# Fused decoder step, end of the expert stage: two pairs added by one-hot products, rows loaded behind the weights, sums and scalings on three engines

## The chip, the cores and the metric

One Trainium2 chip, one of its cores. The metric is the device time of one execution in microseconds (us), smaller is better. The kernel before took 805.71 us (median of 3 runs, 805.52 to 807.05). Engines are named TensorE (PE in the profile, PEld for its weight loads), VectorE (DVE), ScalarE (ACT), GpSimd (POOL) and SyncE (SP, which here only issues DMAs).

## The reference, cut to what matters

One decoder layer for 576 tokens (512 of a prompt, 64 of samples) of width 1024, all fp32. The change touches only its last part: the mixture of experts and the final norm.

```python
def hier_moe(x, lp):                       # 32 experts, each token takes 2 of them
    ...
    combine = ...                          # (tokens, experts): the two weights of each token, else 0
    y = jnp.zeros_like(xt)
    for e in range(N_EXPERTS):
        h = jax.nn.silu(xt @ lp['w_e_gate'][e]) * (xt @ lp['w_e_up'][e])
        y = y + combine[:, e:e + 1] * (h @ lp['w_e_down'][e])
    return y.reshape(shp)
# in the layer, then after it
x = x + hier_moe(rmsnorm(x, lp['norm2_g']), lp)
y = rmsnorm(x, final_norm_g)               # x * rsqrt(mean(x*x) + eps) * gain
```

## The kernel before, in words

The program has one instruction stream per engine, written out by hand, with semaphores between them. Everything up to the router is left alone by the change (some semaphores are merged). At the end stand the expert stage and the final sums.

**Expert stage.** The 32 experts are run as 16 pairs (`NPAIR`), pair i being experts 2i and 2i+1. Each expert of a pair has 64 slots for tokens, so a pair is 128 rows. For pair i: GpSimd gathers the 128 token rows by an indirect DMA (L2625), TensorE turns them (`turn_rows`), multiplies with gate and up weights in two halves (`gate_up(i, 0)`, `gate_up(i, 1)`), ScalarE and VectorE make the hidden values (`gate`, `hidden`), TensorE turns those (`turn_hidden`) and multiplies with the down weights (`down(i)`, into PSUM buffer 3). VectorE copies the result out (`result(i)`, L2404) and GpSimd scatters the 128 rows to a DRAM tensor `expert_rows` (`scatter(i)`, L2634), by (choice, token). The weights, 6 MB per pair, come in chunks of 1 MB through 20 slots of SBUF, issued by SyncE (L511) as `ew_used` says that slots are free. If an expert has more than 64 tokens, an overflow part runs behind `If(overflow(...) > 0)`; in these runs it is skipped.

**The last pair.** Pair 15 isn't scattered. A one-hot matrix `L_SEL` (slot to token) and the weight of each slot `L_W` are made beforehand: VectorE builds matrices (`weigh_slots`, L2416 to L2424), TensorE sums them (`slot_weights`, in `body(13)`), VectorE reads the sum and builds the one-hot matrix (`pick_slots`). The result of `down(15)` is split in a high part (ScalarE, L1679) and a low part (VectorE, L2455), and TensorE adds both to the tokens with `picked`: 4 products of 128x512 for each of the 5 tiles of tokens.

**The end.** The tokens stand in 5 tiles `H_AT[t]` (t = 0 has 64 rows, the others 128). When `scatter(14)` has landed, SyncE issues 10 loads (`load_results`, L554): for each tile the row of its first choice and of its second. VectorE adds them with the weights `R_W0` and `R_W1` (tiles 0 and 1: L2493, L2494, then L2496 adds TensorE's PSUM; tiles 2, 3, 4: TensorE also adds the tile itself and its first choice as products with diagonal matrices, and L2500 adds the second choice). ScalarE squares and sums each tile and takes the root (L1688, L1690), VectorE inverts it and scales the tile by it and by the gain (`finish`, L2510, L2511), and SyncE stores the tile (L581), in the order 0 to 4.

Of the kernel before, what the change touches and what calls it, by code (L numbers as in the profile page):

```python
# [150 lines left out]
M_JUNK = O_A + 14400  # L151
# [16 lines left out]

def piece_of(n, i):

    for off, dims, first, many in SLOTS_E[n % NSLOT]:
# [8 lines left out]
def landed(n):  # L180

    k = n % NSLOT // 2 * 2
    return 16 * (len(SLOTS_E[k]) + len(SLOTS_E[k + 1])) * (n // NSLOT + 1)
# [17 lines left out]
N_MAIN = 6 * NPAIR  # L201
# [26 lines left out]
PE_TILES = {2: 0, 3: 3, 4: 2}  # L228
PICKED = {0: 2, 1: 1, **PE_TILES}
L_HI, L_LO, L_SEL, L_W = M_YO + 1024, M_XGT, M_XG + 1024, R_SS + 13  # L230
# [106 lines left out]
def build(nc, small, ssm, h0, xT, x, memT, mem, wstream, wexp, bias, sbias, skT, sv, mkT, mv, cache_k, cache_v,  # L337
# [18 lines left out]
    with ExitStack() as ctx:  # L356
# [21 lines left out]
        def pat(i, off, *dims, p0=0, pn=P):  # L378
# [14 lines left out]
        x_sq, consts_set, gx_ready, xn_ready = sem("x_sq"), sem("consts_set"), sem("gx_ready"), sem("xn_ready")  # L393
# [8 lines left out]
        qm_sb, memn, memsq, mkv_sb, kmT_sb, thg_sb, zz_ready = (sem(n) for n in (  # L402
            "qm_sb", "memn", "memsq", "mkv_sb", "kmT_sb", "thg_sb", "zz_ready"))
# [5 lines left out]
        ss2, rt_ready, x2_ready, x2T_sb, gate_d, gate_e, m_onehot, oh_ready, idx_ready = (  # L409
            sem(n) for n in ("ss2", "rt_ready", "x2_ready", "x2T_sb", "gate_d", "gate_e", "m_onehot", "oh_ready", "idx_ready"))  # L410
# [13 lines left out]
        ssf, rootf, y_sum, y_done, y_st = (sem(n) for n in ("ssf", "rootf", "y_sum", "y_done", "y_st"))  # L424
        more_ps, diag_w = sem("more_ps"), sem("diag_w")
        cleared, slot_oh, slot_ps, y_half, y_hi, y_lo = (sem(n) for n in (
            "cleared", "slot_oh", "slot_ps", "y_half", "y_hi", "y_lo"))
        out_st = sem("out_st")
# [45 lines left out]
        def _(sp):  # L474
# [28 lines left out]
            def chunk(n, e):  # L503
# [3 lines left out]
                for off, dims, first, many in SLOTS_E[n % NSLOT]:  # L507
# [3 lines left out]
                    sp.dma_start(at(off, *dims), src).then_inc(ew_ready[n % NSLOT // 2], 16)  # L511
# [31 lines left out]
            for n in range(19, N_MAIN):  # L543
                wait_pos(sp, ew_used, n + 1 - NSLOT)
# [5 lines left out]
            def load_results():  # L550
                for t in range(TT):
# [7 lines left out]
            sp.wait_ge(y_sent[0], 16 * (NPAIR // 2))  # L559
            sp.wait_ge(y_sent[1], 16 * (NPAIR // 2 - 1))  # L560
            sp.wait_ge(ew_used, CHUNK_AT["d", NPAIR - 2, 0, 1] + 1)
            load_results()
            with sp.If(overflow(sp) > 0):
                for t in range(TT):
                    sp.wait_ge(ld_row[t], 48 if t < TT - 1 else 64)
                for n in range(N_MAIN, len(CHUNKS)):
# [2209 lines left out]
```

## Time and profile before

| what | us |
|---|---|
| median of the runs | 805.71 |
| the profiled execution's own time | 806.09 |
| its span, first to last instruction | 804.3 |
| TensorE busy (matmul) | 758.0 |
| VectorE busy | 392.3 |
| ScalarE busy | 244.2 |
| GpSimd busy | 74.8 |

A span is what the trace covers; the execution's own time is 1.8 us longer. Matmul records overlap, so a busy TensorE isn't TensorE at its peak. From about 560 us on the page shows 412 to 428 GB/s of DMA in every slice of 20 us, until 764 us; the slice of 764 to 784 us has 304 and the last 236.

### The profile page before, as it was taken

The numbers are of one execution on the slowest core, as the hardware profiler recorded it, in microseconds if no ns is written. First come the engines' busy times: TensorE is split into PE (matmuls) and PEld (weight loads), VectorE is DVE, ScalarE is ACT, GpSimd is POOL, SyncE is SP. The second block draws the span as 40 slices with busy tenths as digits, with TensorE's granted clock in tenths as the row PEclk, the third lists the DMA queues.
The fourth block names the chain that finished last, engine by engine and source line by source line (L and its number), as shares of the span: only waits on it lengthen the run. The fifth ranks groups of instructions, "written<-read, shape, count | busy, mean of one in ns | idle before, by whom it ended". The sixth has DMA issues, their size and how long they took to land.

```text
span 804.3 us, 12111 instructions
## 1 busy us (share of the span) xinstructions
PE 758.0 (94%) x4993; PEld 579.4 (72%) x4993; DVE 392.3 (49%) x734; ACT 244.2 (30%) x429; POOL 74.8 (9%) x104
## 2 busy tenths in 40 slices
PE   8999999999999999999999999999999997778875
PEld 6889999999998766789999989886333332323332
DVE  3599828994632757466244367546121121113237
ACT  1552333213473534552243252112111111100113
POOL 0100022001003010100000010011112211111100
PEclk9999999999999999999999999999999999999998
DMA  9668135623335454210241388269999999999986
GB/s 343 238 190 324 63 109 81 150 77 155 98 133 211 184 215 152 105 53 2 105 161 64 158 325 333 79 268 350 412 421 424 421 421 424 421 422 428 420 304 236
DMA packets 38731, 190.62 MB, mean 237 GB/s; under 512 B 5994, under 2 KB 7546, under 8 KB 22968
## 3 DMA queue, kind: packets, MB, share of 16 engines
q1 hardware_dynamic: 24288, 148.22, 46.7%
q0 software_dynamic: 11200, 34.98, 13.0%
q10 hardware_dynamic: 3184, 6.60, 2.2%
q8 instruction: 41, 0.67, 0.3%
q14 instruction: 18, 0.15, 0.1%
HBM read 176.17 MB, written 21.41 MB: 246 GB/s over the span
## 4 chain that ended last, share of the span: by engine, by line
PE 79%; DMA 11%; ACT 5%; DVE 3%; issue 1%; ACTq 0%; SPq 0%; DVEq 0%
PE ps L611 75%; DMA sb<-in_wexp 10%; PE ps L622 4%; ACT sr L1408 1%; ACT sb L1492 1%; DMA sb<-in_xT 1%; ACT sb L1421 1%; ACT sb L1293 1%; DVE sb L2421 0%; DVE sb L2063 0%; DVE sb L2028 0%; DVE sb L2500 0%; DVE sb L2049 0%; DVE sr L2001 0%; ACT sb L1437 0%
## 5 line engine op out<-in xcount | busy, mean ns | idle before, releaser
L611 PE MATMUL ps<-sb 128*64 128x512 f32 (+16 forms) x2216 | 385.0, 432 | 32.3 <-DMA sb<-in_wexp 21.1
L611 PEld LDWEIGHTS ps<-sb 128*64 128x64 f32 (+6 forms) x2216 | 219.4, 157 | 170.9 <-issue 133.5
L611 PE MATMUL ps<-sr 128*128 128x288 f32 (+2 forms) x2372 | 336.9, 302 | 4.2 <-DVE sr L2455 2.4
L611 PEld LDWEIGHTS ps<-sr 128*128 128x128 f32 x2372 | 320.2, 188 | 14.9 <-issue 8.1
L622 PEld LDWEIGHTS ps<-sb 128*128 128x128 f32 (+3 forms) x405 | 41.8, 140 | 30.0 <-issue 26.5
L2396 DVE SCALAR_TENSOR_TENSOR sb<-sb,ps 128x256 f32<-128x256 f32 x16 | 6.7, 421 | 112.0 <-ACT sb L1660 112.0
L622 PE MATMUL ps<-sb 128*128 128x128 f32 (+3 forms) x405 | 52.6, 269 | 1.5 <-DVE sb L2090 0.6
L2404 DVE COPY sb<-ps 128x1024 f32<-128x1024 f32 x15 | 18.4, 1225 | 61.4 <-PE ps L611 61.4
L2136 DVE TENSOR_TENSOR sr<-sb,sr 128x2048 fp32r<-128x2048 f32 (+1 forms) x15 | 34.7, 2324 | 27.4 <-ACT sr L1403 17.6
L1293 ACT ACTIVATE sb<-ps 128x576 f32<-128x576 f32 (+4 forms) x29 | 22.9, 789 | 70.4 <-PE ps L611 50.4
L2122 DVE SCALAR_TENSOR_TENSOR sb<-sb,ps 128x576 f32<-128x576 f32 x24 | 18.1, 753 | 53.3 <-PE ps L611 53.3
L1655 ACT ACTIVATE sb<-ps 128x256 f32<-128x256 f32 x16 | 6.1, 384 | 106.1 <-PE ps L622 99.8
L2634 POOL DMA_INDIRECT expert_rows<-sb x15 | 15.7, 1047 | 172.1 <-DVE sb L2404 157.6
L1660 ACT ACTIVATE sb<-ps 128x256 f32<-128x256 f32 x16 | 6.1, 383 | 75.2 <-PE ps L611 75.2
L1403 ACT ACTIVATE sr<-sb 128x2048 fp32r<-128x2048 f32 x14 | 26.7, 1912 | 1.9 <-ACT sb L1531 1.2
L1531 ACT ACTIVATE sb<-ps 128x288 f32<-128x288 f32 x24 | 9.6, 408 | 53.7 <-PE ps L611 49.0
L2001 DVE TENSOR_TENSOR sr<-sb,sr 128x2048 fp32r<-128x2048 f32 x6 | 13.7, 2291 | 24.0 <-ACT sr L1408 13.0
L1797 DVE TENSOR_TENSOR sr<-sb,sr 128x2048 fp32r<-128x2048 f32 x10 | 22.9, 2290 | 3.2 <-ACT sr L1315 2.9
L1470 ACT ACTIVATE sb<-sb 128x256 f32<-128x256 f32 (+2 forms) x36 | 16.6, 462 | 24.1 <-DVE sb L2066 24.1
L1315 ACT ACTIVATE sr<-sb 128x2048 fp32r<-128x2048 f32 x10 | 19.0, 1908 | 0.6 <-ACT sb L1293 0.2
L1324 ACT ACTIVATE sb<-ps 128x576 f32<-128x576 f32 x8 | 5.2, 652 | 44.4 <-PE ps L611 44.4
L1650 ACT ACTIVATE sb<-ps 128x1024 f32<-128x1024 f32 x15 | 15.4, 1024 | 9.5 <-PE ps L622 9.5
(275 smaller groups left out, 484.5 us busy)
## 6 DMA issues: line engine op xcount, KB each, us to landing
sb<-in_wexp SPq DMA_DIRECT2D x91, 1024.0 KB, 23.5
sb<-in_wstream SPq DMA_DIRECT2D x33, 1024.0 KB, 5.1
expert_rows<-sb ACTq DMA_DIRECT2D x1, 4608.0 KB, 21.3
sb<-in_mkT POOLq DMA_DIRECT2D x8, 512.0 KB, 9.7
sb<-in_mv POOLq DMA_DIRECT2D x8, 512.0 KB, 6.3
sb<-expert_rows SPq DMA_DIRECT2D x8, 512.0 KB, 8.1
sb<-in_wexp SPq DMA_DIRECT2D x5, 768.0 KB
sb<-in_x SPq DMA_DIRECT2D x4, 512.0 KB, 14.3
```

Source lines behind the costliest of these rows:

```text
L611: return signed(nc.tensor.matmul(*a, **kw))
L622: return signed(nc.tensor.transpose(*a))
L1293: c.free(fn(dst, src, ACT.Copy, **kw), job)
L1315: fn(r32(EARLY_HI[b], WB), at(raw_at(b), (1, WB)), ACT.Copy).then_inc(hi_ready, 1)
L1403: fn(r32(high_at(block), 2048), at(raw_at(b), (1, WB)), ACT.Copy).then_inc(hi_ready, 1)
L1470: fn(at(sc + m * 256, (1, keys)), at(sc + m * 256, (1, keys)), ACT.Exp, bias=at(stat(n, 1) + m, (1, 1)), accum_out=at(stat(n, 3) + m, (1, 1)))
L1650: fn(at(M_XGT, (1, 1024)), pat(0, 0, (1, 1024)), ACT.Copy).then_inc(xT_sb, 1)
L1797: v.tensor_tensor(r32(raw_at(b), WB), at(raw_at(b), (1, WB)), r32(EARLY_HI[b], WB).bitcast(F32), ALU.subtract).then_inc(lo_ready, 1)
L2122: c.free(v.scalar_tensor_tensor(g2, g2, 1.0, pat(pair(name), 0, (512, 2), (1, TH)), ALU.add, ALU.mult), name)
L2136: v.tensor_tensor(r32(src, n), at(src, (1, n)), r32(hi, n).bitcast(F32), ALU.subtract).then_inc(lo_ready, 1)
L2404: v.tensor_copy(at(M_YO + (i % 2) * 1024, (1, 1024)), pat(3, 0, (1, 1024))).then_inc(y_copied, 1)
L2634: pool.indirect_dma_start(out=y_d[:, :], out_offset=bass.IndirectOffsetOnAxis(at(M_IDX + i, (1, 1)).bitcast(U32), 0), in_=at(M_YO + (i % 2 ...
```

## The change

Pairs 14 and 15 (`LAST`) are both added by one-hot products; `scatter(14)` and the copy before it are gone. The row loads then wait for `scatter(13)` only, and come in the order 0, 3, 1, 2, 4. What is summed where also changes: `sum_rows` (tiles 0 and 3) stands on VectorE ahead of the low parts of pair 15; tile 1's rows are scaled by ScalarE and added by GpSimd; tiles 0 and 1 get their final scaling from ScalarE (by the root) and GpSimd (by the gain). Only tile 2 still gets its rows by TensorE's diagonal products. On TensorE the common path stands in its own `If`, and the overflow part behind it. Merged semaphores, moved buffers and slot numbers of the overflow part are left out here.

```diff
@@ sync
             def load_results():
-                for t in range(TT):
+                for t in (0, 3, 1, 2, 4):
...
-            sp.wait_ge(y_sent[0], 16 * (NPAIR // 2))
-            sp.wait_ge(y_sent[1], 16 * (NPAIR // 2 - 1))
-            sp.wait_ge(ew_used, CHUNK_AT["d", NPAIR - 2, 0, 1] + 1)
+            for k in range(2):
+                sp.wait_ge(y_sent[k], 16 * (NPAIR // 2 - 1))
+            sp.wait_ge(ew_used, CHUNK_AT["gu", NPAIR - 2, 1, 1] + 1)
             load_results()
...
-                sp.wait_ge(y_done, t + 1)
+                sp.wait_ge(*((gained, t + 2) if t < 2 else (y_done, t + 1)))
                 sp.dma_start(out_y[WTOK[t]:WTOK[t] + R, :], ...
@@ tensor
             def down(i):
                 pe.wait_ge(hT_sb, i + 1)
-                wait_pos(pe, y_copied, i)
+                wait_pos(pe, y_copied, copies(i - 1))
+                if i == LAST[1]:
+                    pe.wait_ge(y_lo, 2)
...
             def body(i, first, last):
...
-                if i == NPAIR - 3:
-                    slot_weights()
+                if i == NPAIR - 4:
+                    slot_weights(1)
+                if i == NPAIR - 2:
+                    slot_weights(3)
+                if last:
+                    own_rows(2)
                 gate_up(i, 1)
                 if last:
-                    own_rows(2)
+                    pe.wait_ge(y_lo, 2)
+                    for half in range(2):
+                        picked(LAST[0], 2, half)
                     turn_hidden(i)
...
                 down(i1 - 1)
+                for t in range(2):
+                    for half in range(2):
+                        picked(LAST[0], t, half, start=True)
...
+            def sums():
+                pe.wait_ge(y_lo, 3)
+                for t in range(3):
+                    for half in range(2):
+                        if t == 0 and half:
+                            pe.wait_ge(y_lo, 4)
+                        last = picked(LAST[1], t, half, stop=(t < 2))
+                    if t < 2:
+                        last.then_inc(more_ps, 1)
+                pe.wait_ge(diag_w, 1)
+                first_choice(2)
+                for half in range(2):
+                    picked(LAST[0], 3, half, start=True)
+                    last = picked(LAST[1], 3, half, stop=True)
+                last.then_inc(more_ps, 1)
+                pe.wait_ge(y_sum, 1)
+                for half in range(2):
+                    picked(LAST[0], 4, half, start=True)
+                    last = picked(LAST[1], 4, half, stop=True)
+                last.then_inc(more_ps, 1)
@@ scalar
+            def high_rows(j):
+                act.wait_ge(slot_oh, 4 if j == LAST[0] else 6)
+                for half in range(2):
+                    act.wait_ge(*((y_ps, j + 1) if half else (y_half, j - LAST[0] + 1)))
+                    fn(r32(L_HI[j] + half * 512, 512), pat(3, half * 512, (1, 512)), ACT.Copy, scale=at(L_W[j], (1, 1)))\
+                        .then_inc(y_hi, 1)
...
+            high_rows(LAST[1])
+            act.wait_ge(ld_row[1], 48)
+            for k, w in enumerate((R_W0, R_W1)):
+                rows_1 = at(A_WG[1] + k * D, (1, D), pn=WROWS[1])
+                fn(rows_1, rows_1, ACT.Copy, scale=at(w + 1, (1, 1), pn=WROWS[1])).then_inc(scaled, 1)
...
                 fn(ss, ss, ACT.Sqrt, scale=1.0 / D, bias=at(O_EPS, (1, 1), pn=R)).then_inc(rootf, 1)
+                if t in (1, 2):
+                    h = at(H_AT[t - 1], (1, D), pn=WROWS[t - 1])
+                    act.wait_ge(y_done, t)
+                    fn(h, h, ACT.Copy, scale=at(R_SS + 7 + t, (1, 1), pn=WROWS[t - 1])).then_inc(scaled, 1)
@@ vector
             def pairs(i0, i1):
...
+                    if i == NPAIR - 5:
+                        weigh_slots(LAST[0])
                     if i == NPAIR - 4:
                         weight_diagonals()
-                        weigh_slots()
+                    if i == NPAIR - 3:
+                        pick_weight(LAST[0])
+                        weigh_slots(LAST[1])
                     if i == NPAIR - 2:
-                        pick_slots()
-                result(i1 - 2)
+                        pick_tokens(LAST[0])
+                        pick_weight(LAST[1])
+                        pick_tokens(LAST[1])
+                if i1 == NPAIR:
+                    low_rows(LAST[0])
+                else:
+                    result(i1 - 2)
                 hidden(i1 - 1)
+            def add_first(t, rows_landed):     # A_WG = A_WG * R_W0 + H_AT, waits for ld_row[t]
+            def add_second(t):                 # A_WG = A_WG(second) * R_W1 + A_WG
+            def sum_rows(rows_landed):
+                add_first(0, rows_landed)
+                add_second(0)
+                add_first(3, rows_landed)
+                c.settle()
             pairs(0, NPAIR)
+            sum_rows(48)
+            dve.sem_inc(added, 1)
+            low_rows(LAST[1])
...
             def combine(t):
+                if t not in PE_TILES:
+                    dve.wait_ge(more_ps, t + 1)
+                    c.do(v.tensor_tensor(h, pat(PICKED[t], 0, (1, D), pn=R), at(A_WG[t], (1, D), pn=R), ALU.add), y_sum)
+                    return
...
             def finish(t):
                 dve.wait_ge(rootf, t + 1)
-                if t == 0:
+                if t < 2:
+                    c.do(v.reciprocal(ss, ss), y_done)
+                    return
...
+            add_second(3)
             combine(0)
+            add_first(4, 64)
+            add_second(4)
+            finish(0)
+            dve.wait_ge(gained, 1)
             combine(1)
-            finish(0)
-            finish(1)
             combine(2)
             combine(3)
+            finish(1)
+            combine(4)
             finish(2)
-            combine(4)
             finish(3)
             finish(4)
@@ gpsimd
-                    if i > i0:
+                    if i > i0 and i - 1 != LAST[0]:
                         scatter(i - 1)
             pairs(0, NPAIR)
+            rows_1 = [at(A_WG[1] + k * D, (1, D), pn=WROWS[1]) for k in range(2)]
+            for k in range(2):
+                pool.wait_ge(scaled, k + 1)
+                if k:
+                    pool.wait_ge(own_sum, 1)
+                nc.gpsimd.tensor_tensor(rows_1[0], rows_1[k], rows_1[0] if k else at(H_AT[1], (1, D), pn=WROWS[1]), ALU.add)\
+                    .then_inc(gained if k else own_sum, 1)
...
+            pool.wait_ge(ld["gf"], 16)
+            for t in range(2):
+                h = at(H_AT[t], (1, D), pn=WROWS[t])
+                pool.wait_ge(scaled, t + 3)
+                nc.gpsimd.tensor_tensor(h, h, at(M_GF, (1, D), pn=WROWS[t]), ALU.mult).then_inc(gained, 1)
```

## Rows read from the trace of the kernel before

**Rows 1.** The chain that ended last: start us, length us, engine and line.

```profile
746.60 21.92 DMA sb<-in_wexp
768.65 5.57 PE ps L611 x20
779.34 0.76 DVE sr L2455
799.97 1.28 DVE sb L2511
```

**Rows 2.** Stretches: length, busy us (instructions) per engine, PEclk, DMA share, GB/s.

```profile
768.50:771.50 3.00, 2.85 (x14) 1.26 (x16) 0.00 (x0) 0.00 (x0) 0.98 (x1) 1.00 0.99 415
771.50:775.00 3.50, 3.03 (x12) 1.04 (x10) 0.84 (x2) 0.77 (x2) 0.00 (x0) 1.00 0.42 171
775.00:776.50 1.50, 1.50 (x8) 0.54 (x10) 0.00 (x0) 0.00 (x0) 0.00 (x0) 1.00 0.00 0
```

**Rows 3.** Three lots of row loads: ns each, first and last issue, then landing.

```profile
L554 SPq DMA_DIRECT2D sb<-expert_rows x2: 455/526/597, 775.4 to 775.9; - x2
DMA to landing us min/median/max: 3.5/4.6/5.7
...
L554 SPq DMA_DIRECT2D sb<-expert_rows x3: 432/432/1614, 777.2 to 778.1; - x3
DMA to landing us min/median/max: 6.7/7.0/8.9
...
L554 SPq DMA_DIRECT2D sb<-expert_rows x2: 431/456/482, 780.8 to 781.3; - x2
DMA to landing us min/median/max: 8.9/9.7/10.5
```

**Rows 4.** The scatter of pair 13: timeline row, its landing.

```profile
758.60 1.53 POOL L2634 DMA_INDIRECT expert_rows<-sb x1 [12.06 <-DVE sb L2404]
DMA to landing us min/median/max: 8.4/8.4/8.4
```

**Rows 5.** Timeline of GpSimd and VectorE around 541 us; L2275's five instructions (min/median/max ns).

```profile
540.92 2.36 POOL L2613 TENSOR_TENSOR sb<-sb 128x1024 f32<-128x1024 f32 x1 [10.75 <-DVEq L2206]
540.92 0.22 DVE L2271 TENSOR_TENSOR sb<-sb,ps 128x64 f32<-128x64 f32 x1
541.43 2.00 DVE L2275 TENSOR_TENSOR sb<-sb 128x128 f32<-128x128 f32 x1
L2275 DVE TENSOR_TENSOR sb<-sb x5: 283/294/1997, 497.0 to 550.8; 128x128 f32<-128x128 f32 x4, 64x128 f32<-64x128 f32 x1
```

**Rows 6.** VectorE's groups from 776 us on: busy us, mean ns, idle before.

```profile
L2511 DVE SCALAR_TENSOR_TENSOR sb<-sb 128x1024 f32<-128x1024 f32 x4 | 5.1, 1284 | 0.1
L2496 DVE TENSOR_TENSOR sb<-ps,sb 128x1024 f32<-128x1024 f32 x1 | 1.2, 1224 | 0.0
L2510 DVE RECIPROCAL sb<-sb 128x1 f32<-128x1 f32 x4 | 0.6, 160 | 0.3 <-ACT sb L1690 0.3
```

**Rows 7.** ScalarE: square and root of one tile, table load; the copy with a scale (L1641).

```profile
779.56 1.28 ACT L1683 ACT_TABLE_LOAD x1 [0.25 <-issue]
785.47 1.06 ACT L1688 ACTIVATE sb<-sb 64x1024 f32<-64x1024 f32 x1 [4.41 <-DVE sb L2496]
786.65 0.29 ACT L1690 ACTIVATE sb<-sb 64x1 f32<-64x1 f32 x1
L1641 ACT ACTIVATE sb<-sb x1: 1148/1148/1148, 545.0 to 545.0; 128x1024 f32<-128x1024 f32 x1
```

**Rows 8.** The stores of the result.

```profile
DMA to landing us min/median/max: 2.6/2.6/2.9
```

**Rows 9.** TensorE at its slot weights, the next wait for weights, and a stretch between.

```profile
732.20 6.64 PE L611 MATMUL ps<-sb 64*128 64x1 f32 x26 [1.98 <-DVEq L2425]
752.88 3.65 PE L611 MATMUL ps<-sb 128*64 128x512 f32 x16 [0.91 <-DMA sb<-in_wexp]
735.00:736.00 1.00, 1.00 (x4) 0.24 (x2) 0.00 (x0) 0.00 (x0) 0.00 (x0) 0.50 0.99 414
```

More of the change, by code:

```diff
@@ L227, with copies, sent @@
 R_DG = R_SEL[0]
[L228 to L230 removed]
+PE_TILES = {2: 0}
+PICKED = {0: 2, 1: 1, 2: 0, 3: 3, 4: 2}
+LAST = (NPAIR - 2, NPAIR - 1)
+L_HI, L_LO = (dict(zip(LAST, places)) for places in ((O_A + 12544, M_YO + 1024), (O_A + 13568, M_XGT)))
+L_SEL, L_W = (dict(zip(LAST, places)) for places in ((O_X, M_XG + 1024), (R_SS + 5, R_SS + 13)))
+def copies(i):
+    return i + 1 if i < LAST[0] else max(LAST[0], i)
+def sent(i):
+    return i // 2 - (i > LAST[0] and i % 2 == 0)
 L_ONE, L_TMP = O_TH + 2048, R_TB + 32
@@ L1171, in own_rows, with picked, slot_weights @@
                        stop=not start)
-            def slot_weights():
-                pe.wait_ge(slot_oh, 1)
+            def picked(j, t, half, start=False, stop=False):
+                for k, y in enumerate((L_HI[j], L_LO[j])):
+                    last = mm(pat(PICKED[t], half * 512, (1, 512)), r32(L_SEL[j] + WTOK[t], 128), r32(y + half * 512, 512),
+                              start=(start and k == 0), stop=(stop and k == 1))
+                return last
+            def slot_weights(step):
+                pe.wait_ge(slot_oh, step)
                 for t in range(TT):
@@ L1212, in pairs, with first_choice @@
                 down(i1 - 1)
+                for t in range(2):
+                    for half in range(2):
+                        picked(LAST[0], t, half, start=True)
             pairs(0, NPAIR)
-            with pe.If(overflow(pe) > 0):
+            def first_choice(t):
+                pe.wait_ge(ld_row[t], 48 if t < TT - 1 else 64)
+                for half in range(2):
+                    last = mm(pat(PE_TILES[t], half * 512, (1, 512)), at(R_DG + (t - 2) * 128, (1, 128)),
+                              at(A_WG[t] + half * 512, (1, 512)), start=False, stop=True)
+                last.then_inc(more_ps, 1)
[18 more added lines that the diff above has]
+                    last = picked(LAST[1], 4, half, stop=True)
+                last.then_inc(more_ps, 1)
+            many, left = overflow(pe), list(owed)
+            with pe.If(many < 1):
+                sums()
+            with pe.If(many > 0):
+                owed[:] = left
                 own_rows(2, start=False)
+                for t in range(2):
+                    for half in range(2):
+                        picked(LAST[0], t, half, stop=True)
                 pe.wait_ge(oh2_ready, 1)
@@ L2484, in _ @@
                     dve.wait_ge(ld_row[t], 80 if t < TT - 1 else 96)
+                sum_rows(80)
+                add_first(1, 80)
+                add_second(1)
             c = main
```

166 lines of the change are left out of this document (77 added, 89 removed).

## Prediction

> **What bounds the kernel now.** I read the chain of waits first. Up to 768.5 us it lies on the weights' DMA (21.92 us in its last stretch), then TensorE runs the last pair, and from 780 us on it goes through the end's sums to VectorE's last scaling, over at 799.97 + 1.28 = 801.25 us [rows 1]. The last store lands 2.6 us later [rows 8]; the 0.45 us left to 804.3 are its issue and the close. So nothing ahead of the weights' end can gain, unless it reduces what the DMA moves. The stretches say when the DMA is free: it moves 415 GB/s until 771.5 us, 171 until 775 us, and nothing until 776.5 us [rows 2]. It stands still because the row loads are issued only at 775.42 us, after pair 14's scatter. Their landings set when VectorE can begin: the second load of tile 0 was issued at 775.9 us and landed 5.7 us later, at 781.6 us; the second load of the next tile landed at 783.9 (777.2 + 6.7), the third tile's at 787.0 (778.1 + 8.9), the last tile's at 791.8 us (781.3 + 10.5) [rows 3]. From 781.6 to 801.25 us VectorE has hardly a gap. So 19.7 us of VectorE's work, begun by the row loads, is what the change attacks.
>
> **The change, step by step.**
>
> *Row loads.* They now wait for pair 13's scatter, landed at 758.60 + 8.4 = 767.0 us [rows 4], and queue behind the weights and the gain. From 768.5 to 775 us the DMA moved 415 x 3.0 + 171 x 3.5 = 1.84 MB [rows 2]; 0.52 MB of it was pair 14's scatter, now gone. The rest at 415 GB/s takes 3.2 us, so the rows' data begin at about 771.6 us, not 776.5. I move each place in the order 5 us forward: tile 0 at 776.6, tile 3 (second place now) at 778.9, tile 1 (third) at 782.0, tile 4 at 786.8 us. Bounds: 4 us forward if pair 13's scatter is late, 7 us if the queue behind the weights hides the ramp that the first landing shows (3.5 us from issue).
>
> *VectorE ahead of the last low parts.* `sum_rows`, with waits for the rows of tiles 0 and 3, stands in front of `low_rows(15)`: behind these waits queue the low parts, and for those wait TensorE's products. Three instructions of 1.28 us [rows 6] with 0.04 between: 776.6, 779.2 (two of tile 0), 780.6 (first of tile 3); then two low parts of 0.76 [rows 1]: 782.1 us, against 780.10 before. So the low parts are late by 2.0 us, but three of the big sums are done. TensorE's `If` no longer jumps over the overflow part ahead of these products; with the low parts late, TensorE isn't what ends last, so I cost that at nothing.
>
> *The shared work.* GpSimd takes four additions or products of 128x1024 (one of them 64 rows), all with two inputs in SBUF. The only row of that kind took 2.36 us [rows 5], twice VectorE's 1.28. While it ran, VectorE's L2275, also with two SBUF inputs, took 2.00 us, where the others of that line took 0.29, and ended 0.15 us behind GpSimd's. L2271, one input from PSUM, kept to 0.22 us inside the same stretch. So GpSimd holds VectorE's two-SBUF-input instructions for as long as it runs. I take it that it is held by them in turn.
>
> The Trainium skill (SBUF — State Buffer, "Who interferes with whom") says the same of both directions: a VectorE instruction with two SBUF inputs and a GpSimd instruction that reads SBUF exclude each other, and who comes first keeps the port for its whole instruction. The rows agree for one direction (2.00 against 0.29 us); no row shows the other. With both directions the sum below is +3.0 us at VectorE's end; if only GpSimd held VectorE, its own instructions would begin earlier and the sum would be about +2.0.
>
> The series with holds, each end in us:
> - `add_second(3)`: 782.3 to 783.6.
> - Tile 1: rows at 782.0, ScalarE's first scaled copy 1.15 [rows 7] to 783.2; GpSimd's first addition is held to 783.6, ends 786.0; the second 786.15 to 788.5. `combine(0)` runs beside them (PSUM input), 783.6 to 784.9.
> - `add_first(4)`: rows there at 786.8, held to 788.5, ends 789.8; `add_second(4)` 791.1; reciprocal 0.16 [rows 6]: 791.3.
> - `combine(1)` 1.22: 792.6. ScalarE's square to root 786.94 - 785.47 = 1.47 [rows 7]: 794.1. ScalarE scales tile 0, 1.15: 795.3. GpSimd times gain, 2.36: 797.8.
> - `finish(2)` could begin at 797.0, is held to 797.8, ends 799.05. ScalarE's copy of tile 1 was ready at 798.0, so GpSimd comes next: 799.1 to 801.5. `finish(3)` 802.7, reciprocal, `finish(4)` 804.3.
>
> `combine(2)`, `combine(3)` and `combine(4)` lie beside ScalarE's and GpSimd's steps (3.9 us inside 792.6 to 797.0). ScalarE's table load of 1.28 us [rows 7] lies at 784.4 to 786.1, after tile 1's copies: the square of tile 0 waits for it, with no one behind it yet. So VectorE ends at 804.3, not 801.25: +3.0 us. With rows 7 us forward it is 802.3 (+1.0), since the series can't begin before the low parts at 780.1; with 4 us forward 805.3 (+4.0).
>
> *Stores.* SyncE stores in the order 0 to 4, and tile 1 is ready only at 801.5. Four stores of 0.52 MB are then issued within 2.8 us, where 415 GB/s wants 1.26 us each, 5.0 in all. The last lands up to 1.0 us later than the 2.6 behind its issue [rows 8]; below, 0. I take 0.5.
>
> *Slot weights.* Now two steps instead of one, in `body(12)` and `body(14)`. Before, TensorE waited 1.98 us for it and then took 6.64 us, for what includes a burst that takes 3.65, at a granted clock of 0.50 (1.2 GHz) in part: about 5 us in the open. By 752.88 us TensorE was waiting for weights again: lost time made up in 14 us [rows 9]. The second step now falls near 747 us (VectorE's share of it, some 5 us, follows `result(12)`), 21 us ahead of the burst at 768.65 that matters. So 0; the bound above is 2 us at that burst, and of those VectorE's wait for rows (780.6 us) hides most. The moved `own_rows(2)` fits the wait for weights ahead of 768.65.
>
> *Removed:* pair 14's copy of 1.22 us and its scatter, both beside the weights; two of three diagonals; three `own_rows`/`first_choice` steps of TensorE. None is on the new path.
>
> Sum: +3.0 + 0.5 = +3.5 us. Span 804.3 to 807.8, the profiled execution's 806.09 to 809.6; on the scale of the median, 805.71 + 3.5 = **809.2 us**.
>
> **Rivals.**
>
> *B: GpSimd doesn't hold VectorE at the end, and rows come early (the other side).* Place: GpSimd's four instructions. Price of the holds: without them the same series gives `combine(1)` at R + 2.9 and the last scaling at R + 14.0, R being tile 4's landing (from the end of `combine(1)`, ScalarE's four squares and two copies, 8.2 us, and the last scaling, with gaps). With R = 784.8, rows 7 us forward, the end is 798.8, -2.4, stores +0.5: 803.8 us. It decides from R below 785.2 on. For it: `combine` instructions have a PSUM input and are free, and only one pair of rows shows a hold. Against: that pair is clear, and the sum has 3 x 1.28 of VectorE against 2 x 2.36 of GpSimd in one stretch, twice.
>
> *C: no holds, rows as I forecast (R = 786.8).* End 800.8, -0.5, stores +0.5: 805.7 us, no change. VectorE's saved work is given back as a wait for tile 4's rows.
>
> *D: rows or TensorE late.* If the second slot step or a low clock delays pair 13's result, its scatter lands near 770 and `sum_rows` blocks the low parts by 2 to 3 us more. Without holds: 803.3, +2.0, with stores 808.2 us. For it: 5 us in the open [rows 9]. Against: 21 us to make it up, DMA already full.
>
> That the loads don't move forward at all is part of D; the diff leaves no wait that would do that.
>
> **How the numbers follow.** What can be told from no change is 0.2%, 1.6 us. Forecast (holds): 0.57, of it 0.03 within 0.2% (rows early, +1.0 us); its own range 806.7 to 811. B 0.28, faster. C 0.10, same. D 0.05, slower. So faster 0.28, same 0.10 + 0.03 = 0.13, slower 0.54 + 0.05 = 0.59. The upper end is rows 4 us forward (+4.0) with 1.0 for the stores, 810.7, and a little for D: 811.0. The lower end must reach to B: 803.4 leaves out about half of B.
>
> **What would show it.** In the profile after: row loads issued near 767 to 770 us, no still DMA at 775; VectorE's low parts ending near 782; GpSimd's four instructions near 784, 786, 795 and 799 us; VectorE instructions of more than 1.28 us (up to 3.6) at `add_first(4)`, `finish(2)`, `finish(3)`, or gaps there; stores issued close together at the end. I am wrong if GpSimd's and VectorE's two-SBUF-input instructions overlap at full speed, or if tile 4's rows land before 785 us and `combine(1)` starts before 789.

## The result, and the profile after

| | before | after |
|---|---|---|
| median of the runs, us (6 each) | 806.97 | 813.96 |
| lowest to highest, us | 805.52 to 811.18 | 813.51 to 815.45 |
| span of the profiled execution, us | 804.3 | 812.1 |
| VectorE's last scaling ends, us | 801.25 | 807.57 |

The ratio is 1.0071 (95% interval 1.0046 to 1.0097), so 5.7 us slower, where 3.5 us were forecast. The two medians are 7.0 us apart (the six runs of the kernel before spread over 5.7 us), and the profiled span grew by 7.8 us. The direction was right, the size too small: 813.96 lies 3.0 us above the range's end of 811.0. Of the distance to the forecast of 809.2, 1.3 us is the scale, since the kernel before has a median of 806.97 here and had 805.71.

The chain that ended last (start, length, engine and line; compare [rows 1]) now hangs on the last row load, not on TensorE:

```profile
762.20 8.44 DMA expert_rows<-sb
...
775.30 15.76 DMA sb<-expert_rows
791.09 3.02 DVE sb L2522
...
803.31 2.87 DVE sb L2621
```

VectorE's timeline from its first row sum (start, length, line, shapes, idle before and its releaser; L2522 and L2527 are the row sums, L2516 the low parts, L2602 and L2607 the combining, L2621 the final scaling):

```profile
781.60 1.28 DVE L2522 SCALAR_TENSOR_TENSOR sb<-sb 64x1024 f32<-64x1024 f32 x1 [7.07 <-DMA sb<-expert_rows]
...
785.68 1.41 DVE L2516 SCALAR_TENSOR_TENSOR sr<-ps,sb,sr 128x512 fp32r<-128x512 f32 x2 [0.18 <-DVE sb L2522]
787.01 1.28 DVE L2527 SCALAR_TENSOR_TENSOR sb<-sb 128x1024 f32<-128x1024 f32 x1
788.68 1.22 DVE L2602 TENSOR_TENSOR sb<-ps,sb 64x1024 f32<-64x1024 f32 x1 [0.39 <-PE ps L643]
791.09 3.01 DVE L2522 SCALAR_TENSOR_TENSOR sb<-sb 128x1024 f32<-128x1024 f32 x1 [1.19 <-DMA sb<-expert_rows]
...
800.90 1.99 DVE L2621 SCALAR_TENSOR_TENSOR sb<-sb 128x1024 f32<-128x1024 f32 x1
...
803.31 2.87 DVE L2621 SCALAR_TENSOR_TENSOR sb<-sb 128x1024 f32<-128x1024 f32 x1
...
806.29 1.28 DVE L2621 SCALAR_TENSOR_TENSOR sb<-sb 128x1024 f32<-128x1024 f32 x1
```

GpSimd's timeline of the same stretch (the last row holds two instructions, the first of them 2.36 us long):

```profile
787.52 2.99 POOL L2769 TENSOR_TENSOR sb<-sb 128x1024 f32<-128x1024 f32 x1 [23.98 <-ACT sb L1744]
790.66 2.35 POOL L2769 TENSOR_TENSOR sb<-sb 128x1024 f32<-128x1024 f32 x1
799.45 5.64 POOL L2788 TENSOR_TENSOR sb<-sb 64x1024 f32<-64x1024 f32 x2 [6.44 <-ACT sb L1759]
```

Three of VectorE's instructions, 1.28 us long elsewhere, take 3.01, 1.99 and 2.87 us. GpSimd's take 2.99, 2.35, 2.36 and 3.31; 2.36 is the undisturbed length [rows 5]. The 2.99 one began at 787.52 while VectorE's L2527 ran until 788.29, and the 3.31 one at 801.79 while VectorE's scaling ran until 802.89. Each engine waits for the other. The combining instructions, which have a PSUM input, keep to 1.22.

But VectorE's series also begins with rows that are as late as before. The stretches (columns as in [rows 2]):

```profile
765.00:770.00 5.00, 4.91 (x19) 1.58 (x17) 1.50 (x2) 1.38 (x2) 0.00 (x0) 1.00 0.99 410
770.00:773.00 3.00, 3.00 (x16) 1.03 (x12) 0.00 (x0) 0.00 (x0) 0.00 (x0) 1.00 0.64 232
773.00:776.00 3.00, 1.76 (x8) 0.87 (x6) 0.84 (x2) 0.77 (x2) 0.00 (x0) 1.00 1.03 157
776.00:778.00 2.00, 0.88 (x4) 0.40 (x6) 0.00 (x0) 0.00 (x0) 0.00 (x0) 1.00 1.01 234
778.00:786.00 8.00, 4.84 (x22) 2.29 (x18) 4.16 (x4) 1.38 (x2) 0.00 (x0) 0.96 1.02 400
```

SyncE's row loads and stores, and TensorE around the end of the weights:

```profile
770.69 5.04 SPq L584 DMA_DIRECT2D sb<-expert_rows  x10
801.84 6.17 SPq L613 DMA_DIRECT2D out_y<-sb  x5
```

```profile
748.88 6.64 PE L643 MATMUL ps<-sb 64*128 64x1 f32 x26 [1.43 <-DVEq L2494]
...
777.12 3.65 PE L643 MATMUL ps<-sb 128*64 128x512 f32 x16 [2.10 <-DMA sb<-in_wexp]
...
786.49 5.49 PE L643 MATMUL ps<-sr 128*128 128x512 f32 x12 [3.64 <-DVE sr L2516]
```

The loads are issued at 770.69 instead of 775.42 us, yet tile 0's rows land at 781.6 as before, the last tile's at 791.1 instead of 791.8. (A tile's landing is that of its second load.) From 773 to 778 us the DMA is busy all the time (share 1.03, 1.01) and moves 157 and 234 GB/s: the packets are slow, not missing. Counted from the trace's DMA records, a 4 KB packet of the rows takes 159 ns as a rule and 424 on average in 774 to 776; the two packets left of the weights, 8 KB each, take 857 on average (831 and 884) instead of 309. So the last weights are late too: TensorE's last down products wait 2.10 us for them and begin at 777.12, before at 774.91.

### The profile page after: what moved, and what is told of

The parts are those of the page before. It is cut to its first block, busy times and chain, and to the rows that moved or that the text cites. A ratio compares the mean times of both kernels' runs of the same rounds, so it can differ in the third digit from the quotient of the medians.

```text
span 812.1 us, 12178 instructions
## 1 busy us (share of the span) xinstructions
PE 762.8 (94%) x5007; PEld 583.1 (72%) x5007; DVE 402.2 (50%) x755; ACT 249.7 (31%) x435; POOL 85.3 (11%) x107
## 4 chain that ended last, share of the span: by engine, by line
PE 77%; DMA 11%; ACT 5%; DVE 5%; issue 1%; SPq 1%; ACTq 0%; DVEq 0%; POOLq 0%
PE ps L643 73%; DMA sb<-in_wexp 7%; PE ps L654 4%; DMA sb<-expert_rows 2%; DMA expert_rows<-sb 1%; DVE sb L2490 1%; ACT sb L1547 1%; DMA sb<-in_xT 1%; ACT sb L1476 1%; ACT sb L1348 1%; SPq L584 1%; DVE sb L2621 1%; ACT sr L1463 0%; ACT sb L1525 0%; DVE sb L2473 0%
## 5 line engine op out<-in xcount | busy, mean ns | idle before, releaser
L643 PE MATMUL ps<-sb 128*64 128x512 f32 (+17 forms) x2210 | 383.8, 435 | 27.9 <-DMA sb<-in_wexp 15.0
L643 PE MATMUL ps<-sr 128*128 128x288 f32 (+2 forms) x2392 | 342.4, 303 | 5.0 <-DVE sr L2516 3.6
L643 PEld LDWEIGHTS ps<-sr 128*128 128x128 f32 x2392 | 324.3, 189 | 17.4 <-issue 5.5
```

Source lines behind the costliest of these rows:

```text
L643: return signed(nc.tensor.matmul(*a, **kw))
```

## The experiments

Ratios are to the kernel before, with their 95% intervals. Landings and last ends are from the profiled executions.

**e1: GpSimd's instructions cut to 16 of 1024 columns** (the rest of those sums and scalings is left out).

```diff
-h = at(H_AT[t], (1, D), pn=WROWS[t])
+h = at(H_AT[t], (1, 16), pn=WROWS[t])       # and the two additions the same way
```

> The changed kernel, with GpSimd's four instructions at the end on 16 of their 1024 columns (the other columns of tiles 0 and 1 miss a sum or the gain). Theory H (GpSimd's length and its holds of VectorE cost): VectorE's first sum of tile 4 takes 1.28 us instead of 3.01, its scalings of tiles 2 and 3 take 1.28 instead of 1.99 and 2.87, its last one ends near 804.9 us instead of 807.6, the stores no longer bunch; the time falls by about 3.2 us against the changed kernel, to some 811. Rival (the end is bound by ScalarE's squares and roots, holds are hidden): under 1 us.

Measured 810.84 us, ratio 1.0039 (1.0015 to 1.0063), against 1.0071: 2.6 us back, and nine of its ten runs lie below all six of the changed kernel. VectorE's row sum and the first of its final scalings:

```profile
795.80 1.28 DVE L2522 SCALAR_TENSOR_TENSOR sb<-sb 128x1024 f32<-128x1024 f32 x1 [1.54 <-DMA sb<-expert_rows]
...
803.89 1.28 DVE L2621 SCALAR_TENSOR_TENSOR sb<-sb 128x1024 f32<-128x1024 f32 x1
```

All are 1.28 us again. From the last rows to the last scaling's end it is 13.2 us (795.80 to 808.98), after the change 16.5: 3.3 us is what the holds cost. Only this length can be compared: the profiled execution is the slowest of the ten, and in it everything from the last weights on lies 4 to 5 us later (the forecast had the last end at 804.9).

**e2: both slot steps one pair earlier** (scatter 13 at 758.92 instead of 762.20, the loads issued at 767.30).

```diff
-                if i == NPAIR - 4:      slot_weights(1)
-                if i == NPAIR - 2:      slot_weights(3)
+                if i == NPAIR - 5:      slot_weights(1)
+                if i == NPAIR - 3:      slot_weights(3)
```

> The changed kernel, with both slot steps one resp. one pair earlier (pair 14 in the body of pair 11, pair 15 in the body of pair 13, where the kernel before had its only one). Theory S (the second slot step near the end made pair 13's scatter late, and with it the row loads): pair 13's scatter is issued near 758.6 us instead of 762.2, the row loads near 767 instead of 770.7, tile 4's rows land near 788.5 instead of 791.1, the time falls by about 2.5 us. Rival (the slow phase of the DMA at tile 0's 64-row loads, beside the last weights, sets the landings whatever the issue): tile 4's rows land within 1 us of before, the time falls by under 1 us.

Measured 815.25 us, ratio 1.0107 (1.0060 to 1.0155): nothing gained. The stretches and TensorE's last down products (the first 4 of 16):

```profile
770.00:773.00 3.00, 3.00 (x14) 1.17 (x11) 0.00 (x0) 0.38 (x1) 0.00 (x0) 1.00 1.05 246
773.00:780.00 7.00, 4.19 (x13) 1.51 (x14) 0.84 (x2) 0.38 (x1) 0.00 (x0) 0.70 1.03 216
```

```profile
776.93 1.97 PE L643 MATMUL ps<-sb 128*64 128x512 f32 x4 [2.55 <-DMA sb<-in_wexp]
```

Issued 3.4 us earlier, the rows of tile 0 land at 782.5 and of tile 4 at 792.1, later than after the change: the slow stretch only begins earlier and catches more of the weights (their 8 KB packets take 502 ns on average from 770 to 772 us, 39 of them). The rival came out: I had expected tile 4's rows at 788.5. My reason "the scatter is late" fell.

**e3: the row loads wait until the last weights have landed.**

```diff
             sp.wait_ge(ew_used, CHUNK_AT["gu", NPAIR - 2, 1, 1] + 1)
+            sp.wait_ge(ew_ready[slot_of(N_MAIN - 1) // 2], landed(N_MAIN - 1))
             load_results()
```

> The changed kernel, with the row loads issued only when the last weights have landed. Theory W (the early row loads slow the last weights and gain nothing themselves): the last weights land near 774.5 us instead of 777.1, the down products of pair 15 begin near 775 instead of 777.1, the rows are issued near 775, tile 4's rows land near 791.5, and the time stays within 1 us of the changed kernel. Rival (the early issue did bring the rows forward, they are late for another reason): tile 4's rows land near 795 and the time rises by 3 us or more.

Measured 812.19 us, ratio 1.0057 (1.0033 to 1.0081), 1.1 us under the changed kernel by the ratios, which isn't clear of their intervals. The weights are in time, and the last rows land at 790.9 although issued 3.1 us later (773.80). In the trace VectorE ends 1.8 us earlier (805.77), since GpSimd's additions start earlier too and hold `add_first(4)` less (1.42 us instead of 3.01):

```profile
774.77 3.65 PE L644 MATMUL ps<-sb 128*64 128x512 f32 x16 [0.47 <-ACT sb L1711]
```

**e4: the low parts ahead of the row sums.**

```diff
+            low_rows(LAST[1])
             sum_rows(48)
             dve.sem_inc(added, 1)
-            low_rows(LAST[1])
```

> The changed kernel, with the low parts of pair 15 ahead of the sums of tiles 0 and 3 on VectorE, so that they no longer wait for rows. Theory R (tile 4's rows and the holds set the end; the low parts stand before a wait anyway): low parts end near 782.3 us instead of 787.1, TensorE's last products start there, VectorE's first sum of tile 4 still begins at 791, the time is within 1 us. Rival (VectorE blocking its low parts is what costs): the time falls by 3 us or more.

Measured 815.18 us, ratio 1.0105 (1.0075 to 1.0136): no gain, rather a loss. So TensorE's 3.64 us of waiting for the low parts was not what set the time. The trace says little beside that: it is of the slowest of the six executions (818.97 us), in which the last weights were late by more (down products at 781.90), and the low parts ended at 788.6 instead of the 782.3 that I had expected.

**e5: tile 0's loads on 128 partitions** (0.5 MB more; tile 0 gets the rows of other tokens).

```diff
-                    R = WROWS[t]
+                    R, r0 = P, WTOK[t] if t else T - P
```

> The changed kernel, with tile 0's two row loads on 128 partitions instead of 64 (tile 0 then gets rows of other tokens, and 0.5 MB more is moved). Theory P (loads that write only half of the partitions make every packet slow while they run, the last weights' too): no stretch of 150 to 260 GB/s in the row phase, the last weights land in time (the down products of pair 15 begin below 775.5 us instead of 777.1), tile 4's rows land near 786 instead of 791.1, the time falls by 3 us or more, to some 810. Rival (the slow packets come from where the rows lie in DRAM, or from the queue): the slow stretch stays, tile 4's rows land at 791 or later, the time is within 1 us or higher.

Measured 810.34 us, ratio 1.0029 (1.0012 to 1.0046): 3.4 us back. The stretches:

```profile
770.00:773.00 3.00, 3.00 (x16) 1.24 (x12) 0.33 (x1) 0.39 (x1) 0.00 (x0) 1.00 1.00 414
773.00:776.00 3.00, 2.27 (x12) 0.83 (x12) 0.51 (x2) 0.38 (x1) 0.00 (x0) 1.00 1.02 416
776.00:780.00 4.00, 4.00 (x20) 1.85 (x14) 2.79 (x3) 1.38 (x2) 0.00 (x0) 1.00 1.04 421
```

The slow stretch is gone, the down products begin at 774.51, tile 0's rows are used at 777.14, and the last land at 786.9, which the prediction had at 786.8. VectorE ends at 803.15. In this trace the loads were also issued earlier than after the change (767.00 instead of 770.69), but that isn't the reason: e2 issued them as early (767.30), and there tile 0 landed at 782.5 and tile 4 at 792.1, here at 777.1 and 786.9.

**e6: the kernel before, TensorE's usual path in an `If` of its own,** so that it doesn't jump over the overflow part.

```diff
+            with pe.If(many < 1):
+                sums()
```

> The kernel before, with one part of the change alone: TensorE's common path in its own If, so that no jump over the overflow part stands ahead of the last one-hot products. Theory J (the jump is what kept TensorE idle for 2.4 us): those products begin near 780.2 us or earlier instead of 780.96, right behind the low parts, and TensorE ends about 0.8 us earlier; VectorE starts by the row loads at 781.6 either way, so the time falls by 0.3 to 0.8 us. Rival (the idle time is the register load and the wait): no move at all.

Measured 806.18 us, ratio 0.9983 (0.9958 to 1.0007), so no move that is clear of the noise. The first products on the low parts start without a gap and take 3.21 us for 12 (before: from 780.96 on, 4.58 us for 12), and TensorE then waits 1.96 us for rows:

```profile
780.12 3.21 PE L611 MATMUL ps<-sr 128*128 128x512 f32 x12
...
787.92 3.67 PE L611 MATMUL ps<-sb 128*128 128x512 f32 x8 [1.96 <-DMA sb<-expert_rows]
```

**e7: e3, and VectorE does GpSimd's and ScalarE's share of the sums and scalings.**

```diff
-                pool.wait_ge(scaled, t + 3)
-                nc.gpsimd.tensor_tensor(h, h, at(M_GF, (1, D), pn=WROWS[t]), ALU.mult).then_inc(gained, 1)
...
+            add_first(1, 48)
+            add_second(1)
...
             finish(1)
+            add_first(4, 64)
+            add_second(4)
             combine(4)
```

Tile 4's sums also move: they stand behind the scaling of tile 1, where its rows have long landed.

> The changed kernel with rows behind the last weights (as the third experiment), and with the work of GpSimd and ScalarE's scaled copies at the end given back to VectorE: it adds tile 1's rows and scales tiles 0 and 1 itself; nothing is left out. Theory H (GpSimd's help costs more than it gives): 2 to 3 us below the third experiment (812.2), some 809.5, with all of VectorE's instructions at 1.2 to 1.3 us and no wait for tile 4's rows. Rival (VectorE is now the bound and needs the help): above 812 us.

Measured 809.20 us, ratio 1.0013 (0.9991 to 1.0034), its median 3.0 us under e3's and 3.5 us by the ratios. In the trace the last scaling ends 0.6 us earlier (805.19 against 805.77), and the span is 2.0 us shorter (808.3 against 810.3), since the stores no longer bunch. VectorE alone, with four more instructions of 1.2 to 1.3 us, is faster than the three engines, though the later place of tile 4's sums has a share in that which isn't separated: e3 waits 3.50 us for their rows, e7 not at all.

**e8: e3 with the split of the sums of the kernel before** (tiles 2 to 4 with own rows and first choice on TensorE, the rest on VectorE).

```diff
-PE_TILES = {2: 0}
+PE_TILES = {2: 0, 3: 3, 4: 2}
```

> Candidate for a better version: the changed kernel's one-hot products for pairs 14 and 15, its TensorE branch and rows behind the last weights, but the end's sums shared as before (TensorE adds tiles 2, 3, 4 and their first choices; VectorE the rest and all scalings; GpSimd nothing; rows in the order 0 to 4; the low parts behind tile 0's first sum). By the durations of the traces VectorE's last scaling ends near 800.7 us against 801.25 of the kernel before: 0.5 us faster than before, some 805.8. Rival (two pairs by one-hot products cost TensorE more than they give): 1 us or more slower than before.

Measured 807.25 us, ratio 0.9991 (0.9973 to 1.0008), as before. VectorE waits 2.87 us for TensorE at tile 3: here TensorE sets the end, and the last scaling ends at 802.21 instead of the 800.7 that I had expected.

**f1 to f4: a source pattern that failed.** They were to keep tile 0's source rows and change the width alone.

```diff
-                        sp.dma_start(at(A_WG[t] + k * D, (1, D), pn=R),
-                                     y_d[k * T + WTOK[t]:k * T + WTOK[t] + R, :]).then_inc(ld_row[t], 16)
+                        src = bass.AP(y_d, (k * T + WTOK[t]) * D, [[0, P // WROWS[t]], [D, WROWS[t]], [1, D]])
+                        sp.dma_start(at(A_WG[t] + k * D, (1, D)), src).then_inc(ld_row[t], 16)
```

> The kernel before with one edit: each of tile 0's two row loads writes 128 partitions instead of 64, from the same 64 rows of the scratch table, read twice (the second copy lands on partitions 64 to 127, which nothing reads; 0.5 MB more). This keeps the source rows and the row order, so it separates the destination from the source. Theory P (a load that writes half of the partitions holds all transfers): no slow stretch at 776 to 780 us; the stretch moves over 380 GB/s, tile 0's rows have landed by about 779.9 instead of 781.6, and the last rows by 789.5 to 790.0 instead of 791.8. If the source rows were the cause (the same 64 rows, freshly written), the slow packets stay and the landings stay within 0.5 us of 781.6 and 791.8. The time hardly follows in either case, since TensorE's products for tiles 2 to 4 set the end in the kernel before (VectorE waits 0.93 us for them at 794.36): 0 to 0.8 us less, ratio about 0.9995. Rival: the rows do set the end, and it is 1.5 us less.

> The changed kernel without GpSimd's sums and scalings (VectorE and nobody else does them), as in e7, but with the rows asked for at once behind the scatters and tile 0's two row loads widened to 128 partitions from the same 64 rows. Theory (the slow stretch and the holds are the whole loss, and they add): rows begin to be used at 777.1 to 777.5 instead of 778.9, last rows by 787; VectorE's 24.5 us of work then end near 802.0 instead of 805.2. Against e7 (ratio 1.0013) 3.0 us less: ratio about 0.998. The series is VectorE alone, so it ends 0.5 to 1 us after that of the kernel before (801.25) in the trace. Rival: TensorE's products for tiles 1 to 4 become late once the rows are early, VectorE waits for them over 1.5 us in sum, and no more than 1.5 us is gained against e7.

> As e8 (both pairs by one-hot products, the split of the sums between TensorE and VectorE as in the kernel before), but the rows asked for at once behind the scatters, and tile 0's two row loads widened to 128 partitions from the same 64 rows. Theory: the rows come about 2 us earlier (last by 787 instead of about 791), and it is worth nothing, since TensorE's unbroken products from 775.4 to 796.9 set the end: VectorE waits 4 to 5 us for TensorE at tile 3 instead of 2.87, and the last scaling ends within 0.5 us of e8's 802.21. Ratio 0.999, as e8. Rival: rows still set the end, and it is 1.5 us less or more.

> As f3_e8_wide, but tile 4 is taken off TensorE's share: its own rows and first choice (8 plain products, 3.6 us) are left to VectorE as two more 1.28 us sums, put where VectorE otherwise waits. Theory: VectorE's busy time from its first row sum becomes 22.2 us without a long wait, from 777.5 on, and the last scaling ends at 799.3 to 800.0, 1.3 to 2 us before that of the kernel before (801.25): ratio 0.9976 to 0.9985, under both kernels. Rival: something else ends last (TensorE's products for tile 4 at 795 or later, or ScalarE's squares), VectorE waits over 2 us, and the time is that of the kernel before, ratio 0.9995 to 1.000.

Measured 829.11, 828.09, 828.41 and 826.41 us (ratios 1.0275, 1.0256, 1.0258, 1.0234, each within 0.004). Two stretches of f1, and VectorE's first row sum:

```profile
776.00:784.00 8.00, 6.73 (x29) 3.69 (x25) 1.50 (x2) 2.86 (x4) 0.00 (x0) 1.00 0.15 49
784.00:802.00 18.00, 1.25 (x5) 0.56 (x3) 0.00 (x0) 0.00 (x0) 0.00 (x0) 0.63 0.84 243
```

```profile
803.74 1.28 DVE L2492 SCALAR_TENSOR_TENSOR sb<-sb 64x1024 f32<-64x1024 f32 x1 [23.89 <-DMA sb<-expert_rows]
```

From 778 to 780 us and from 780 to 782 there are 26 packets each, of 159 ns: 26 x 0.159 / 2 is about 2, so two engines at work, where the plain loads keep the share of all 16 near 1. Only tile 0's pattern has two blocks, but the other loads come behind it with packets of 202 to 290 ns on average from 784 to 802 us. The Trainium skill (DMA: Bandwidth & Descriptors, "Rules for kernel authors") says that an outermost dimension of fewer than 16 confines a transfer to at most that many engines; the trace agrees (2 blocks, 2 engines). On the question of the width these four say nothing.

**g1: the kernel before, tile 0's loads as one plain block of 128 rows** (the scratch table is 64 rows longer).

```diff
-    y_d = nc.dram_tensor("expert_rows", [PAIRS, D], F32)
+    y_d = nc.dram_tensor("expert_rows", [PAIRS + P - WROWS[0], D], F32)
...
+                        r0 = k * T + WTOK[t]
+                        sp.dma_start(at(A_WG[t] + k * D, (1, D)), y_d[r0:r0 + P, :]).then_inc(ld_row[t], 16)
```

> The test that f1_before_wide missed: its source pattern (2 blocks of the same 64 rows) left tile 0's loads to 26 packets in 2 us, where a plain load of rows has about 200. Here each of tile 0's loads is one plain block of 128 rows of the scratch table (its own 64 and the 64 behind them; the table is 64 rows longer, and these are cleared with the rest), on 128 partitions. All else is the kernel before. Theory P (half of the partitions): no slow stretch at 776 to 780 us, tile 0's rows landed by about 779.9 instead of 781.6, the last rows by 789.5 to 790.0 instead of 791.8; time 0 to 0.8 us less (TensorE's products for tiles 2 to 4 set the end), ratio about 0.9995. If the 64 rows themselves are slow to read, the landings stay within 0.5 us of those of the kernel before. Rival on the time: the rows set the end, 1.5 us less.

Measured 808.80 us, ratio 1.0025 (1.0004 to 1.0045): slower, against my -0.8 to 0. Mean ns of the rows' 4 KB packets, from the DMA records:

| us | 776 to 778 | 778 to 780 | 780 to 782 |
|---|---|---|---|
| before | 241 | 280 | 183 |
| g1 | 225 | 168 | 163 |

So the same 64 rows, read with the next 64 into 128 partitions, are not slow to read; the first 2 us, in which the DMA starts from standstill, are slow in both. But the landings didn't move: tile 0's rows land at 781.8 (before 781.6, expected 779.9) and the last at 791.7 (before 791.8, expected 789.5 to 790.0). By my own rule that was the sign for "the 64 rows themselves are slow". The packets say otherwise, and g2 below: here twice the bytes arrive in the same time, and the 0.5 MB more, 1.3 us at 415 GB/s, eat what the width gives. In a kernel whose rows start from standstill the padding thus gains nothing. TensorE's products behind the low parts start at 781.99 instead of 780.96, which sets the end: VectorE waits for them twice (0.92 and 0.86 us), and its last scaling ends 1.0 us later. These products start 1.6 us after the second low part, where before it was 0.9. The DMA records show what goes with it: a 16 KB packet of the instruction queue that ends at 779.31 in the kernel before, 780.44 in g1 and 778.07 in f1, and the products start 1.65, 1.55 and 1.53 us behind it, in f1 even before the second low part is done. e6 has no such packet there and no gap. That TensorE waits for this packet is inferred from these four traces, and why it comes later in g1 is open.

**g2: f2 with plain blocks of 128 rows. g3: f4 with them. g4: g3 with tile 0's loads as they were and the wait of e3.** g3 leaves the own rows and the first choice of tiles 2 and 3 alone on TensorE:

```diff
-PE_TILES = {2: 0, 3: 3, 4: 2}
+PE_TILES = {2: 0, 3: 3}
...
             finish(0)
+            add_first(4, 64)
+            add_second(4)
```

> The changed kernel without GpSimd's sums and scalings (as e7), rows asked for at once behind the scatters, tile 0's loads as one plain block of 128 rows each. Theory (slow stretch and holds are the whole loss, and they add): the first row sum of VectorE at 777.1 to 777.5 instead of 778.9, last rows by 787, VectorE's 24.5 us of work end near 802.0 instead of 805.2; ratio about 0.998, against 1.0013 of e7. Rival: VectorE then waits for TensorE over 1.5 us in sum and at most 1.5 us is gained against e7.

> Both pairs by one-hot products, TensorE takes the own rows and the first choice of tiles 2 and 3 only, VectorE all else, no GpSimd; rows asked for at once, tile 0's loads as plain blocks of 128 rows. VectorE's work from its first row sum is 22.2 us without a long wait, from 777.5 on: the last scaling ends at 799.3 to 800.0, 1.3 to 2 us before that of the kernel before (801.25); ratio 0.9976 to 0.9985. Rival: TensorE's products for tile 4 (795 or later) or ScalarE's squares end later, VectorE waits over 2 us, ratio 0.9995 to 1.000.

> As g3_split_rows128 but with tile 0's loads as they were (64 rows on 64 partitions) and the rows asked for once the last weights have landed, as in e3. Theory (the split is worth 1 us or so by itself, the rows' loads the rest): first row sum at 779.2, last scaling at 801.0 to 801.6, ratio 0.9990 to 1.0000; g3 is 1.3 to 2 us faster than this one. Rival: VectorE's series is not bound by the rows, g3 and g4 within 0.5 us of each other.

| | median us | ratio | first row sum | last scaling ends |
|---|---|---|---|---|
| g2 | 807.56 | 1.0005 (0.9984 to 1.0026) | 777.39 | 802.14 |
| g3 | 805.70 | 0.9978 (0.9959 to 0.9998) | 777.77 | 800.77 |
| g4 | 808.31 | 1.0014 (0.9996 to 1.0032) | 779.95 | 803.82 |

g3, its DMA at the end of the weights and its last scaling:

```profile
773.00:776.00 3.00, 2.27 (x10) 0.97 (x11) 0.84 (x2) 0.62 (x2) 0.00 (x0) 1.00 1.02 411
```

```profile
799.49 1.28 DVE L2601 SCALAR_TENSOR_TENSOR sb<-sb 128x1024 f32<-128x1024 f32 x1
```

In g2 the second load of tile 0 lands at 777.4 and tile 4's at 787.2, at 411 and 421 GB/s from 770 to 776 us, with tile 0's own source rows: so it wasn't the rows. g2 ended within 0.2 us of the forecast in the trace (3.05 us ahead of e7, whose profiled execution was 1.0 us slower than its median), while its ratio moved by only 0.0008 against e7's; the two weren't timed side by side, and their intervals leave room for up to 3 us. g3 beats the changed kernel and, just clear of the noise, the kernel before (1.8 us by the ratio); its last scaling ended at 800.77, not at 799.3 to 800.0. g4 missed its forecast (ratio 0.9990 to 1.0000, last scaling at 801.0 to 801.6). g3's median is 2.6 us under g4's, timed beside it. That is the price of the loads' form and of the later issue together (775.36 instead of 769.71), not of the form alone, and in the trace g4 was already 1.4 us behind at the last down products (776.50 instead of 775.12).

## Why the prediction was right in direction and wrong in size

In the profiled executions the change cost 7.8 us of span, the sum said 3.5. By its steps:

| step | forecast | measured |
|---|---|---|
| tile 4's rows, landed | 786.8 | 791.1 |
| from there to the last scaling's end | 17.5 | 16.5 |
| what follows it, against before | +0.5 | +1.5 |

**Row loads: the step that failed.** "I move each place in the order 5 us forward" took every byte behind the weights at 415 GB/s. The last place moved by 0.8 us (791.84 to 791.06), the first by nothing, outside my bounds of 4 to 7 us. Loads that write 64 partitions make a slow stretch, and the change moved it onto the last weights. It was in the trace of before: [rows 2] ended at 776.5, and I didn't ask for the stretch behind it (columns as there):

```profile
776.50:780.00 3.50, 2.07 (x10) 0.43 (x6) 1.41 (x2) 1.82 (x3) 0.00 (x0) 1.00 0.93 228
```

Yet the 5.7 us to tile 0's second landing [rows 3] lay open. I called them a ramp, which they are only in part (g1). e5 shows what the width does (-3.4 us by the ratios, landing 786.9), e2 beside it that an earlier issue without the width gains nothing, and g2 that the source rows aren't it. The Trainium skill (SBUF — State Buffer, "Door 1: The DMA port swizzle") says that partitions 0 to 63 reach only 8 of the 16 DMA ports, no more than the first 32 do. The runs agree roughly with a halving (157 to 246 GB/s against 415), and that page would have given this rival; I had weighed only its other section. e5 is also the change as I had drawn it, rows in time and holds in place: 2.3 us slower than the kernel before by the ratio, where the sum said 3.5. So the direction wasn't luck.

**What bounded the kernel before: misread.** I had VectorE's 19.7 us begun by the row loads. The chain that ended last runs through TensorE's products instead,

```profile
780.96 13.31 PE ps L611 x36
```

and VectorE waits 0.93 us for them at 794.36. So by this trace rows that came earlier could have gained that kernel little by themselves. The sum for the changed kernel doesn't rest on it: TensorE's share is smaller there, and VectorE waits for it once in this stretch, 0.39 us.

**Holds: right.** e1 prices them at 3.3 us in the trace, 2.6 by the ratios. The forecast's series from tile 4's rows on was 1.0 us too long, spread over its steps (0.3 us of it by the end of ScalarE's copy of tile 0). The rule of the Trainium skill on both directions (SBUF — State Buffer, "Who interferes with whom") is borne out: GpSimd's 2.99 and 3.31 us against 2.36.

**Low parts and TensorE: cost taken at nothing, right.** Forecast 2.0 us later, the low parts were 7.0 us later (787.09 instead of 780.09), since the rows ahead of them were late. TensorE had waited 3.64 us, and its granted clock was 0.50 (1.2 GHz) from 786 to 791 us. But e4, without that wait, gained nothing.

**Slot weights: taken at nothing, and no run shows a cost.** In the trace of the change scatter 13 is issued 3.6 us later (762.20 instead of 758.60). But e5 and g2 have both steps in the same places and issue it at 758.59 and 758.90. What differs in the traces is the granted clock, 0.77 in 715 to 730 us and 0.89 in 745 to 760 after the change, 0.89 and 1.00 in e5; that this made the scatter late isn't tested. It didn't matter either: e2 issued early and gained nothing, and in g3 the loads were issued only 1.0 us ahead of the change's and the last rows came 3.5 us earlier.

**Stores: mis-sized.** The last two stores landed 4.2 and 4.1 us after issue, not 2.6 [rows 8]: +1.5 us where I had 0.5.

**Rivals.** B and C needed GpSimd and VectorE to run side by side; they don't. D had the rows late by way of the scatter. Its sign came true (the scatter landed at 770.64, D said near 770), but that wasn't what made the rows late: e2 had the scatter early and the rows late all the same.

## What to carry to other kernels

Before moving a transfer next to a critical one, look at what it does to the DMA's rate where it runs now: a share near 1 with half the GB/s was here a load that fills half of the partitions, and it slowed the weights in flight beside it. Where such a load runs beside something that matters, pad it to 128 partitions by a plain block of rows (e5, g2), not by a source pattern of two blocks (f1 to f4); where nothing critical runs beside it, the padding gained nothing (g1). Additions and scalings with two SBUF inputs weren't shared by giving them to GpSimd: the two engines took turns, and GpSimd's turn is the longer one (2.36 us against 1.28).

## What the runs showed of the hardware that I had not expected

- TensorE's products behind the skipped `If` start 0.9 us after the second low part in the kernel before, and 2.5 us after the first, which is all that the first of them need. In e6 they start at once.
